# One 512-column matmul for the high and low activations in a convolved projection, its halves joined by VectorE

## What is computed

```
def conv_ffn(h, w_up, conv_w, conv_b, w_down):
    u = h @ w_up
    up = jnp.pad(u, ((0, 0), (1, 1), (0, 0)))
    u = up[:, :-2] * conv_w[0] + up[:, 1:-1] * conv_w[1] + up[:, 2:] * conv_w[2] + conv_b
    gate, val = jnp.split(u, 2, axis=-1)
    return (jax.nn.silu(gate) * val) @ w_down
```

## Time and profile before

| | us |
|---|---|
| median of 3 runs (1951.63 to 1952.05) | 1951.73 |
| the profiled execution | 1952.31 |
| its span | 1950.5 |
| TensorE busy | 1925.8 |
| VectorE busy | 1322.7 |
| ScalarE busy | 1101.4 |
| GpSimd busy | 166.3 |

### The profile page before, as it was taken

The page is one execution under the profiler, slowest core; times in us unless marked ns, Lnnn a source line. Parts: engine busy times, 40 slices in busy tenths (PEclk is TensorE's granted clock), DMA queues, the critical chain, the costliest instruction groups (busy, mean ns, idle before and its releaser), DMA issues.

```text
span 1950.5 us, 29009 instructions
## 1 busy us (share of the span) xinstructions
PE 1925.8 (99%) x11352; PEld 1661.3 (85%) x11352; DVE 1322.7 (68%) x2282; ACT 1101.4 (56%) x1852; POOL 166.3 (9%) x248
## 2 busy tenths in 40 slices
PE   9999999999999999999999999999999999999999
PEld 8878998887899988888987788888888897878887
DVE  5866976576697657556787875555555688886554
ACT  6666765476676554445567554444444566655442
POOL 1110222011012100000012200000000001210000
PEclk9999999999999999999999999999999999999999
DMA  8434556543455655555543355555555544345553
GB/s 300 139 105 141 190 182 234 182 139 112 140 170 188 197 181 193 185 187 176 175 157 107 108 178 189 185 183 191 180 189 187 182 153 150 100 132 183 189 184 123
DMA packets 90680, 329.83 MB, mean 169 GB/s; under 512 B 10032, under 2 KB 10416, under 8 KB 90288
## 3 DMA queue, kind: packets, MB, share of 16 engines
q1 hardware_dynamic: 90544, 327.98, 51.1%
HBM read 326.89 MB, written 1.05 MB: 168 GB/s over the span
## 4 chain that ended last, share of the span: by engine, by line
PE 88%; DVE 6%; ACT 4%; issue 1%; DMA 1%; SPq 0%; DVEq 0%; ACTq 0%
PE PS L83 85%; PE PS L86 3%; DVE WL L98 2%; ACT TMP L95 1%; DVE TMP L108 1%; ACT WH L92 1%; DVE SM L114 1%; DMA RAW<-wts 1%; ACT M L92 0%; ACT M L95 0%; SPq L80 0%; ACT TMP L92 0%; DVE X L98 0%; DVE SM L108 0%; DVE SM L98 0%
## 5 line engine op out<-in xcount | busy, mean ns | idle before, releaser
L98 DVE TENSOR_TENSOR WL<-RAW,WH 128x1024 fp32r<-128x1024 f32 (+1 forms) x609 | 745.6, 1230 | 476.3 <-ACT WH L92 469.8
L92 ACT ACTIVATE WH<-RAW 128x1024 fp32r<-128x1024 f32 (+1 forms) x609 | 641.3, 1057 | 533.5 <-PE PS L83 526.6
L83 PE MATMUL PS<-WH,GH 128*128 128x512 f32 (+1 forms) x1008 | 397.2, 394 | 4.9 <-DVE GL L98 4.7
L83 PE MATMUL PS<-WH,GL 128*128 128x512 f32 (+1 forms) x1008 | 388.5, 385 | 0.0
L83 PE MATMUL PS<-WL,GH 128*128 128x512 f32 (+1 forms) x1008 | 388.2, 385 | 0.0
L83 PE MATMUL PS<-WH,HH 128*128 128x512 f32 (+1 forms) x832 | 315.8, 380 | 0.0
L83 PE MATMUL PS<-WL,HH 128*128 128x512 f32 (+1 forms) x832 | 312.2, 375 | 0.0
L83 PE MATMUL PS<-WH,HL 128*128 128x512 f32 (+1 forms) x832 | 312.2, 375 | 0.0
L83 PE MATMUL PS<-GH,WH 128*128 128x256 f32 x928 | 264.5, 285 | 0.8 <-issue 0.4
L83 PE MATMUL PS<-GL,WH 128*128 128x256 f32 x928 | 262.6, 283 | 0.0
L83 PE MATMUL PS<-GH,WL 128*128 128x256 f32 x928 | 262.6, 283 | 0.0
(11 more groups left out here) (151 smaller groups left out, 2151.8 us busy)
## 6 DMA issues: line engine op xcount, KB each, us to landing
RAW<-wts SPq DMA_DIRECT2D x607, 512.0 KB, 4.1
M<-bias SPq DMA_DIRECT2D x4, 512.0 KB, 10.8
M<-bias SPq DMA_DIRECT2D x1, 2048.0 KB, 9.6
X<-x SPq DMA_DIRECT2D x2, 512.0 KB, 5.7
TMP<-mem SPq DMA_DIRECT2D x1, 1024.0 KB, 12.0
out<-X SPq DMA_DIRECT2D x4, 256.0 KB, 3.8
CST<-cst SPq DMA_DIRECT2D x1, 714.0 KB, 9.8
RAW<-wts SPq DMA_DIRECT2D x2, 256.0 KB, 5.9
```

The source lines that it names most:

```text
L83: return Issued(self.eng and self.eng.matmul(o, l, r, start=first, stop=last, skip_group_check=share))
L92: return Issued(self.eng.activation(o, i, f, scale=scale))
L98: return Issued(self.eng and self.eng.tensor_tensor(o, a, b, op))
```

## The change

**Layout.** The high and the low activations lie in one tensor, `GX[:, 0]` and `GX[:, 1]` (and `HX` in the same way), so that one access pattern can stream both.

**The projection, tiles 6 to 43.** A new helper `fm_halves` does in each of 8 steps one matmul of 512 columns (high weights x [high, low] activations, into a whole PSUM bank: the left half gets high x high, the right half high x low) and one of 256 columns (low weights x high activations, into the left half). The right half must now be added to the left one. ScalarE copies it to TMP (`rest(n)`, last in turn n), VectorE adds the left half in TMP (`join(n - 1)`, first in turn n), and identity and taps read the sum from TMP. TAPPED moves so that from tile 11 on it is d + 3, and the loops have 51 turns for 49. The bank is free after `join`.

**GpSimd** takes over silu(gate) x value from VectorE. Its order in a turn is a product, then a low part two turns later than its product.

**The decays.** `CUM` and `HEAD` have all 128 rows. `HEAD`'s further rows are zeros from the constants, and `CUM`'s further rows are what WDHL holds there.

The diff, without the lines that only follow from the names:

```diff
+        HX = sb("HX", [128, 2, KD, S], FR)
+        HH, HL = HX[:, 0, :, :], HX[:, 1, :, :]
+        GX = sb("GX", [128, 2, FF, S], FR)
+        GH, GL = GX[:, 0, :, :], GX[:, 1, :, :]
...
-        CUM = WDHL[0:48, :]
-        HEAD = sb("HEAD", [48, 16], FR)
+        CUM = WDHL[:, :]
+        HEAD = sb("HEAD", [128, 16], FR)
...
-        TAPPED = [6, 6, 7, 7, 8, 9, 9, 10, 11, 11, 12, 12, 13, 14] + [d + 1 for d in range(14, 2 * FF)]
+        TAPPED = [6, 6, 7, 7, 8, 9, 9, 10, 11, 12, 13] + [d + 3 for d in range(11, 2 * FF)]
...
+            def fm_halves(key, acts, xs, allowed=WHOLE):
+
+                ps = take(key, allowed)
+                for i, (ah, _, made_by) in enumerate(acts):
+                    h, o = at[0] // 8, at[0] % 8 * 128
+                    e.wait_ge(lo, h)
+                    e.wait_ge(low_of(made_by), made_by)
+                    wh, wl = WH[:, h % HS, o:o + 128], WL[:, h % HS, o:o + 128]
+                    last = i == len(acts) - 1
+                    e.mm(ps[:, :], wh, xs[:, :, i, :], i == 0, False)
+                    m = e.mm(ps[:, 0:S], wl, ah, False, last)
...
                 for n in range(6, 2 * FF):
-                    fm_tile(("up", L, n), whole)
+                    fm_halves(("up", L, n), whole, GX[:, :, 14:22, :])
...
-                    e.mm(ps[:, 0:256], HEAD[:, h:h + 1].to_broadcast([48, 128]), CUM, True, True).then_inc(
+                    e.mm(ps[:, 0:256], HEAD[:, h:h + 1].to_broadcast([128, 128]), CUM, True, True).then_inc(
...
-                        e.wait_ge(tile, key)
-                        e.act(ACT.Identity, conv_c(n), bank(key)[:, 0:S], scale=w, bias=col(pb + P_CB + ch)).then_inc(
+                        e.wait_ge(made, key)
+                        e.act(ACT.Identity, conv_c(n), conv_t(n)[:, 1:257], scale=w, bias=col(pb + P_CB + ch)).then_inc(
                             ready, ("id", L, n))
+
+                def rest(n):
+
+                    key = ("up", L, n)
+                    e.wait_ge(tile, key)
+                    if n >= 8:
+                        e.wait_ge(made, ("c", L, n - 8))
+                    e.act(ACT.Copy, conv_t(n)[:, 1:257], bank(key)[:, S:2 * S]).then_inc(aout, ("rest", L, n))
...
                 def high(p):
-                    e.wait_ge(made, ("gv", L, p))
+                    e.wait_ge(multiplied, ("gv", L, p))
...
-                for n in range(2 * FF + 5):
+                for n in range(2 * FF + 7):
...
                     for p in pair_at(n, 0, 1):
                         gate(p)
+                    if 6 <= n < 2 * FF:
+                        rest(n)
...
                     else:
-                        ps = bank(key)
-                        e.stt(c[:, 1:S], ps[:, 0:S - 1], col(w), c[:, 1:S], ALU.mult, ALU.add).then_inc(made)
+                        u = conv_t(n)
+                        e.stt(c[:, 1:S], u[:, 1:S], col(w), c[:, 1:S], ALU.mult, ALU.add).then_inc(made)
                         e.wait_ge(made)
-                        e.stt(c[:, 0:S - 1], ps[:, 1:S], col(w + 88), c[:, 0:S - 1], ALU.mult, ALU.add).then_inc(
-                            made, ("c", L, n), key)
-                def product(p):
...
+                        e.stt(c[:, 0:S - 1], u[:, 2:S + 1], col(w + 88), c[:, 0:S - 1], ALU.mult, ALU.add).then_inc(
+                            made, ("c", L, n))
+
+
+                def join(n):
+
+                    key, u = ("up", L, n), conv_t(n)[:, 1:257]
+                    e.wait_ge(aout, ("rest", L, n))
+                    e.tt(u, u, bank(key)[:, 0:S], ALU.add).then_inc(made, key)
...
-                for n in range(2 * FF + 5):
+                for n in range(2 * FF + 7):
+                    if 6 <= n - 1 < 2 * FF:
+                        join(n - 1)
                     if n < 2 * FF:
                         lows(("up", L, n))
...
-                    for p in pair_at(n, 1, 1):
-                        product(p)
...
-                for p in range(FF):
-                    gh, gl = G(1, p)
-                    e.wait_ge(ahi, ("g", L, p))
-                    e.tt(gl, conv_t(2 * p + 1)[:, 260:516], gh.bitcast(F32), ALU.subtract).then_inc(glo, ("g", L, p))
+                for n in range(2 * FF + 7):
+                    for p in pair_at(n, 1, 1):
+                        c = conv_t(2 * p + 1)[:, 260:516]
+                        e.wait_ge(ready, ("silu", L, 2 * p))
+                        e.wait_ge(made, ("c", L, 2 * p + 1))
+                        e.tt(c, conv_t(2 * p)[:, 260:516], c, ALU.mult).then_inc(multiplied, ("gv", L, p))
+                    for p in pair_at(n, 1, 3):
+                        gh, gl = G(1, p)
+                        e.wait_ge(ahi, ("g", L, p))
+                        e.tt(gl, conv_t(2 * p + 1)[:, 260:516], gh.bitcast(F32), ALU.subtract).then_inc(
+                            glo, ("g", L, p))
```

More of the change, by code:

```diff
@@ L199, in build @@
         gated = signal("gated")
+        multiplied = signal("multiplied")
         BANK, HALF = {}, {}
@@ L549, in fm_tile @@
                     m = e.mm(ps, wl, ah, False, last)
+                    at[0] += 1
+                    done = [key] if last else []
+                    if at[0] % 8 == 0:
+                        done.append(("half", h))
+                    if done:
+                        m.then_inc(tile, *done)
+                HALF[key] = h
+            def fm_halves(key, acts, xs, allowed=WHOLE):
[8 more added lines that the diff above has]
+                    m = e.mm(ps[:, 0:S], wl, ah, False, last)
                     at[0] += 1
@@ L2070, in block2 @@
                 if L == 0:
-                    e.copy(HEAD[:, :], CST[0:48, C_HD:C_HD + 16]).then_inc(made, "head")
+                    e.copy(HEAD[:, :], CST[:, C_HD:C_HD + 16]).then_inc(made, "head")
                 e.wait_ge(ready, ("wdh", L))
```

## The result

The changed kernel is slower: 1961.18 us median (1960.84 to 1962.31, 4 runs) for 1951.89 (1951.63 to 1952.15) of the kernel before on the same chip, a ratio of 1.0048 with a 95% interval of 1.0036 to 1.0060. The profiled execution took 1960.86 us, its span is 1959.0, 8.5 more than before.

A forecast was written before the change was run, and what follows sets the result against it. TensorE was taken as the bound, busy 1925.8 of 1950.5 us. Stream -8.3, decays -3.1 and waits at the projections' ends +3.8 sum to -7.6: 1944.7 for the profiled execution, 1944.1 median, range 1940.0 to 1952.5.

The forecast's parts named there:

- The backlog: VectorE's lateness from the projection's first turns, put at 1.9 us at its end, making TensorE wait 1.9 us a layer.
- 0.6 us of delay in a pair: GpSimd's two operations would delay VectorE by 0.6 us in a pair of tiles, between bounds of 0 and 1.0.
- T + 0.95: T is the down projection's start; without a backlog VectorE would end turn 43's taps about 0.95 us after it.
- the whole reserve: Time between a low half's end and when TensorE wants it in the projection, some 5.5 us.
- The stream's gain: Projection tiles 6 to 43: 608 steps save 0.0137 us each with 512-column matmuls, 8.3 us less.
- rival (a): VectorE and GpSimd become the bound, TensorE stops within the projection, 7.5 us lost a layer: 1955.3 us; chance 0.12.
- The decays: Full-height decay matmuls: 14 pairs save 0.2 us and 2 save 0.38, less 0.4 for waits, 3.1 us less.
- the 0.10: Decays: the saving on the first full matmul behind a pair, part of the 0.2 us a pair.
- (b): Backlog kept in full, reserve spent only at the projection's end, 5.5 us a layer: 1951.3, no change; chance 0.11.
- Rival (c): The two-piece stream in the projection is no cheaper, a tile stays at 2.89 us: 1950.6, no change; chance 0.07.
- (d): No wait at all at the end of the projection: 1940.3 us; chance 0.08.
- over 4 us: Sign of being wrong: the TensorE gap at the projection's end is missing or longer than 4 us.

The follow-up runs named there:

- Experiment 2: The changed kernel with product and low part of g both back on VectorE, GpSimd idle in the projection; 1945.23 us, ratio 0.9966.
- experiment 7: The changed kernel with both operations on VectorE, next halves in turns 44, 46, 48, and high and low side by side as one piece; 1944.33 us.
- experiments 4 and 8: 4: kernel before with only the 512-column stream, 1947.81 us. 8: changed kernel, both mends, each tile's 512-column matmuls first, then its 256-column ones, 1941.79 us.
- experiment 6: The changed kernel with product and low part on VectorE and the next halves of weights written in turns 44, 46 and 48; 1944.16 us, ratio 0.9960.
- experiment 3: The changed kernel with the product alone back on VectorE, GpSimd keeping the low part; 1955.43 us, ratio 1.0014.

## Why the prediction was wrong

It said 1944.1 us, within 1940.0 to 1952.5, and gave slower 0.12. Measured are 1961.2. The profiled execution is 16.2 us over the forecast of 1944.7 for it. By the steps of the forecast:

**The backlog was mis-sized, +8.3.** This is the step that failed. The prediction had the prices of VectorE and GpSimd right and took 0.6 us of delay in a pair, because "only some of GpSimd's operations fall on such a boundary" and because the product would lie partly beside the join. The runs show 1.0. VectorE has no pauses in these rows, so the waiting low part comes in at a boundary each time, and the product starts under the join (262.82 under 262.59) but outlasts it, so that the subtraction behind it (262.92) is the one held. With 0.6 the backlog of the first tiles is worked off slowly; with 1.0 a pair is 5.75 against 5.65, so that it is kept and grows by 0.1 a pair. Turn 43's taps end at T + 6.8 where the forecast's sum without a backlog had T + 0.95: a backlog of 5.9, not 1.9, which is the whole reserve. From there to the end of the low half it is 7.8 us, for 7.25 in the middle of the forecast. 4.0 and 0.5 more, less 0.2 by which the half is wanted later, make a wait of 6.2 where 1.9 stood. Experiment 2 shows the same step from the other side: without the delays a pair is 5.44, the last join starts 1.6 us behind its tile's last matmul instead of 7.0, and 0.2 us of the wait is left in each layer.

**The stream's gain was mis-sized, +4.2.** The row was known to be missing ("No row shows such a stream"), and the upper bound was taken. The doubt was put in the wrong place: two pieces cost nothing (experiment 7), the alternation costs most of the 0.006 us a step (experiments 4 and 8). The gain is 4.1 for 8.3. It also lengthens TensorE's pair to 5.65, which made VectorE's overload smaller than rival (a) had it.

**The clock behind the gap wasn't in the sum, +4.1.** A gap was priced at its length. The rows show half clock behind it, for some 5 us in the first layer and some 2 in the second.

**The decays were nearly right, with some luck.** -3.1 forecast, -3.0 measured, alone and in the whole; but 0.4 of it is the stretch of half clock that the kernel before had there, so that the term itself is about -2.5. Of the places, the first matmul of full height behind a pair starts 0.24 before the third (1091.22 and 1091.46), with nothing of the 0.10 on it:

```profile
1090.88 0.51 PE L83 MATMUL PS<-WDHL,HEAD 128*128 128x256 f32 x2
1091.22 0.40 PE L83 MATMUL PS<-HX,WH 128*128 128x256 f32 x2
1091.46 0.28 PE L83 MATMUL PS<-HX,WL 128*128 128x256 f32 x1
```

The three terms are 16.6. With 0.1 in the second block and 0.8 of small waits, less the 1.4 (0.6 + 0.4 + 0.4) that lie where the change has nothing, they make 16.1 of the 16.2.

**The rivals.** What happened is (b) by its course (the reserve spent at the end alone, 6.1 us a layer where it says 5.5) for the reason that (a) names (full delays, past the point of 0.78 us a pair). (a)'s long stops within the projection did not come, since the longer tile left an overload of 0.1 a pair, not 0.24. (b) gave 1951.3 only because it booked the full stream and no clock; with the two measured terms, and 1.1 for its own shorter wait, it is 1951.3 + 4.2 + 4.1 + 1.1 = 1960.7. Rival (c) had the size of the stream between it and the forecast, (d) could not be reached: without any wait the change gives 1944.2 (experiment 6). Of the signs that the prediction named for being wrong, "over 4 us" at the end is what came; the 512-column starts, at 0.236 in the mean, lie between its 0.227 and 0.24. The chance of 0.12 for (a) was too low for a case whose price was a full one in every row that it read; the argument against it was a guess about timing that no row supported.

## What to carry to other kernels

Price work handed to GpSimd from a full VectorE by what it delays there. In these kernels that was 0.5 us for an operation of 256 elements that VectorE does in 0.34, each time that VectorE's neighbouring instructions read two operands from SBUF, while taps that read one from PSUM went free. Before you load an engine up to its last per cent, look at the next place where its output is wanted behind the loop: three halves written between the last turns, rather than behind them, were worth 13 us. And in a run of matmuls, keep equal lengths together: grouping them gave 1.9 us more at no cost.

## What was not expected of the hardware

**The clock behind a gap.** In the changed kernel TensorE stood for 6.2 us and then ran at a granted clock of 0.50, the level of 1.2 GHz, from the first matmul on: 0.59 us, then 0.43 for each, for some 5 us in the first layer and 2 in the second. In experiment 3 it stood for 3.4 us. In its first layer the first five steps behind the gap were 0.34 and then 0.23 to 0.25 us, nearly those of full clock, before 0.43 set in (in order of time; the third row is two matmuls); in its second layer 0.59 and 0.43 came at once:

```profile
316.59 0.50 PE L83 MATMUL PS<-WH,GX 128*128 128x512 f32 x1 [3.28 <-DVE WL L98]
316.93 0.40 PE L83 MATMUL PS<-WL,GX 128*128 128x512 f32 x1
317.17 0.63 PE L83 MATMUL PS<-WH,GX 128*128 128x512 f32 x2
317.64 0.45 PE L83 MATMUL PS<-WL,GX 128*128 128x512 f32 x1
```

Behind its two gaps 20 matmuls start 0.42 to 0.43 apart, more than the 16 behind the longer ones. So the gaps of 3.4 us cost 1.8 and 2.9 us of clock beside their own length, and those of 6.2 and 5.9 cost 2.6 and 1.5: for the time that follows, the shorter gap was no cheaper. It also varies between runs of the same kernel. Of experiment 3's ten, the three with a mean granted clock of 0.999 took 1952.5 to 1953.1 us and the two with 0.996 took 1956.6 and 1957.9. The Trainium skill says in TensorE: Matmul & The Clock Gate, Wait — 56ns, not 53.3ns?, that a matmul of 512 columns on the cold array takes 426.7 ns from start to start. The rows agree, with 0.43; at full clock they have 0.227, where the page has 0.216.

**Lengths that alternate.** In turn, matmuls of 512 and 256 columns take 0.236 + 0.117 = 0.353 us from start to start, whether the moving operand is in one piece or in two (experiments 6 and 7); among their own kind they take 0.227 and 0.120.
